# A one-core transformer step: rows of x saved earlier, state and gate transfers moved off a hand-over, a row chain spread over three pairs

## The reference, cut to what matters

```
x = x_sample + position table          (latent tokens only)
h = rms_norm(x) * (1 + scale1) + shift1         scale, shift, gate = silu(c) @ w_ada + b_ada
z = h @ w_in                                    branches A, B, C and their merge gates
y = (sig(gA)*A + sig(gB)*B + sig(gC)*C) @ w_out
x = x + gate1 * rms_norm(y)
h = rms_norm(x) * (1 + scale2) + shift2
a, b = h @ w_ffn_in ;  x = x + gate2 * rms_norm((silu(a) * b) @ w_ffn_out)
```

## Time and profile before

| | us |
|---|---|
| median of 3 runs | 1740.62 (1739.48 to 1744.54) |
| the profiled execution | 1741.52 |
| its span, first to last instruction | 1739.7 |
| PE busy | 1692.2 (97%) |
| DVE busy | 992.7 (57%) |
| ACT busy | 628.8 (36%) |
| POOL busy | 222.5 (13%) |
| granted TensorE clock, mean | 0.993 |

### The profile page before, as it was taken

How to read it: one execution, slowest core, us unless ns; L and a number is a source line. 1 busy time by engine, 2 the same in 40 slices (tenths; PEclk the granted TensorE clock), 3 DMA queues, 4 the chain that set the end, 5 groups by cost and what they waited for, 6 DMA issues and landing times. The chain is left out here.

```text
span 1739.7 us, 24679 instructions
## 1 busy us (share of the span) xinstructions
PE 1692.2 (97%) x9558; PEld 1601.8 (92%) x9558; DVE 992.7 (57%) x1674; ACT 628.8 (36%) x1102; POOL 222.5 (13%) x340
## 2 busy tenths in 40 slices
PE   6899999999999999999999899999999999999996
PEld 3799999989999999998988799999999999888885
DVE  5654443343444444456978886555555553589885
ACT  6311212242322222234667563222222222454452
POOL 1400001322222233311000000000000000000000
PEclk9999999999999999999999999999999999999998
DMA  9655445664455556679876322221122226567683
GB/s 349 234 176 186 163 150 198 227 201 140 165 173 172 186 190 206 198 253 274 265 234 192 141 101 81 76 67 70 60 75 76 76 76 193 152 198 240 187 277 124
DMA packets 155579, 295.74 MB, mean 170 GB/s; under 512 B 12761, under 2 KB 91932, under 8 KB 155466
## 3 DMA queue, kind: packets, MB, share of 16 engines
q1 hardware_dynamic: 111600, 162.69, 28.8%
q0 software_dynamic: 27536, 91.31, 16.0%
q10 hardware_dynamic: 16336, 40.29, 6.3%
HBM read 226.46 MB, written 67.82 MB: 169 GB/s over the span
## 5 line engine op out<-in xcount | busy, mean ns | idle before, releaser
L669 PE MATMUL bank<-h_hi,w_hi 128*128 128x384 f32 x1080 | 370.8, 343 | 7.5 <-DVE h_lo L2658 3.6
L671 PE MATMUL bank<-h_hi,w_lo 128*128 128x384 f32 x1080 | 362.0, 335 | 0.0
L670 PE MATMUL bank<-h_lo,w_hi 128*128 128x384 f32 x1080 | 361.7, 335 | 0.0
L1972 DVE TENSOR_TENSOR w_lo<-raw,w_hi 128x1024 fp32r<-128x1024 f32 x154 | 187.3, 1220 | 143.9 <-ACT w_hi L1482 143.8
L669 PEld LDWEIGHTS bank<-h_hi,w_hi 128*128 128x128 f32 x1080 | 203.4, 188 | 12.3 <-DVE h_lo L2658 5.8
L670 PEld LDWEIGHTS bank<-h_lo,w_hi 128*128 128x128 f32 x1080 | 203.6, 188 | 0.1
L671 PEld LDWEIGHTS bank<-h_hi,w_lo 128*128 128x128 f32 x1080 | 203.1, 188 | 0.0
L1482 ACT CAST w_hi<-raw 128x1024 fp32r<-128x1024 f32 x154 | 159.3, 1052 | 98.8 <-PE bank L671 43.2
L670 PE MATMUL bank<-w_lo,a_hi 128*128 128x512 f32 x352 | 136.9, 389 | 0.0
L671 PE MATMUL bank<-w_hi,a_lo 128*128 128x512 f32 x352 | 136.9, 389 | 0.0
L669 PE MATMUL bank<-w_hi,a_hi 128*128 128x512 f32 x352 | 136.9, 389 | 0.0
(11 more groups left out here) (358 smaller groups left out, 3375.7 us busy)
## 6 DMA issues: line engine op xcount, KB each, us to landing
raw<-in_w_stream SPq DMA_DIRECT2D x144, 512.0 KB, 4.5
z_scratch<-z_st ACTq DMA_DIRECT2D x44, 576.0 KB, 2.9
raw<-in_w_stream SPq DMA_DIRECT2D x90, 256.0 KB, 4.5
raw<-in_w_ada SPq DMA_DIRECT2D x35, 512.0 KB, 4.4
mg<-z_scratch ACTq DMA_DIRECT2D x24, 576.0 KB, 5.3
a_raw<-f_scratch SPq DMA_DIRECT2D x44, 256.0 KB, 3.8
a_raw<-f_scratch SPq DMA_DIRECT2D x22, 320.0 KB, 3.6
zt<-z_scratch POOLq DMA_DIRECT2D x27, 256.0 KB, 4.2
```

What stands on the lines that cost most here:

```text
L669: pe.matmul(out, a_hi, b_hi, start=start, stop=False)
L670: pe.matmul(out, a_hi, b_lo, start=False, stop=False)
L671: return pe.matmul(out, a_lo, b_hi, start=False, stop=stop)
L1972: dve.tensor_tensor(w_lo[:, slot], raw[:, slot], w_hi[:, slot].bitcast(F32), ALU.subtract).then_inc(s_wlo, 1)
```

## The change

- SP's first stream load of unit 1 keeps its place in time but is written into turn 0, and right behind it SP itself issues the nine stores of `x_in` (`x_stores`). POOL's nine stores and a wait before them are gone; POOL still waits for them to land.
- `mg_load(0)` and `mg_load(1)` move from part 2 of `hm`, ahead of pieces 2 and 3 of `mx`, to parts 3 and 4.
- The two stores of new_C move from POOL's place ahead of `mx_load(2)` to e2(0), beside those of new_n.
- `x_add(3g+1)` moves from the first unit of e1(g+1) to the end of e2(g).
- In e2(2) DVE splits the first feed-forward unit before `combine(0)` instead of after it, and makes `s_low(0)` before `t_low(4)`.
- The row chain of tiles 6 to 8 (`x_add`, `x_square`, `x_rstd`, `x_norm`) is spread from pair 0 over pairs 0 to 2, and POOL's `x1_store` of them comes behind the first stores of f.

```diff
+            def x_stores():
+                sp.wait_ge(s_padd, 2 * (LAT // P))
+                for c in range(NT):
+                    sp.wait_ge(s_xin[c], 16)
+                    sp.dma_start(xp_dram[c], x_in[:, c]).then_inc(s_xps, 16)
...
                     load((n0 + 2) % RAW, w_ada[bass.ds(i * (2 * RAW) + (ADA_FIRST + 2 * u + 1), 1)])
+                    if first and u == 0:
+                        sp.wait_ge(s_unit, n0 + 3 - RAW + 1)
+                        load((n0 + 3) % RAW, w_stream[1:2])
+                        x_stores()
...
-                        mg_load(0)
-                        mg_load(1)
+                    if part in (3, 4):
+                        mg_load(part - 3)
                     for k in MX_PARTS[part]:
                         mx_piece(0, k)
...
-                    if j == 0:
-                        x_square(6)
+                    if j == 1:
                         x_norm(6)
                     elif j == 2:
+                        x_norm(8)
                         h2_out(6)
...
-                    if j == 0:
+                    if j == 1:
                         x_square(7)
...
-                    if j == 0:
+                    if j == 1:
                         x_norm(7)
                     act.wait_ge(s_pv, vector_step(j, "c12"))
                     act.activation(v1[:, :], v1[:, :], ACT.Silu).then_inc(s_pact, 1)
-                    if j == 0:
-                        x_square(8)
-                        x_norm(8)
+                    if j < 2:
+                        x_square(6 + 2 * j)
...
-                    if g and c == 0:
-                        x_add(m + 1)
...
-                    if g < NG - 1 or k not in (3, 4):
+                    if g < NG - 1 or k not in (3, 4, 5):
                         split(n + AHEAD, n + AHEAD)
...
                             x_add(3 * g)
+                            x_add(3 * g + 1)
...
                             t_low(i)
+                        split(n + 2 + AHEAD, n + 2 + AHEAD)
                         combine(0)
                     elif k == 5:
+                        s_low(0)
                         t_low(4)
-                        s_low(0)
...
-                        x_add(6)
                     dve.wait_ge(s_pact, scalar_step(j, "s1"))
...
+                    if j == 1:
+                        x_rstd(6)
+                        x_add(7)
+                    elif j == 2:
+                        x_rstd(8)
...
-                    if j == 0:
-                        x_rstd(6)
-                        x_add(7)
...
-                    if j == 0:
-                        x_add(8)
+                    if j == 1:
                         x_rstd(7)
...
-                    if j == 0:
-                        x_rstd(8)
+                    if j < 2:
+                        x_add(6 + 2 * j)
...
-            pool.wait_ge(s_xr, NT)
-            for c in range(NT):
-                pool.dma_start(xp_dram[c], x_in[:, c]).then_inc(s_xps, 16)
             pool.wait_ge(s_xps, 16 * NT)
...
             hm_load(8)
-            for d in range(2):
-                pool.dma_start(new_C[0, 0, d].rearrange("h k v -> k h v"), st_ctx[:, d, :, 0:DH]).then_inc(s_new, 16)
             mx_load(2)
...
                     for d in range(2):
+                        pool.dma_start(new_C[0, 0, d].rearrange("h k v -> k h v"), st_ctx[:, d, :, 0:DH]).then_inc(s_new, 16)
...
-                    if j == 0:
-                        for m in range(6, 9):
-                            x1_store(m)
                     f_store(0, j, c21[:, :], s_pv, vector_step(j, "f1"))
                     f_store(1, j, v2[:, :], s_pv, vector_step(j, "f2"))
+                    if j == 0:
+                        x1_store(6)
+                    elif j == 1:
+                        x1_store(7)
+                        x1_store(8)
```

More of the change, by code:

```diff
@@ L788, in z1_turn @@
                     n0 = ADA_FIRST + 3 * u
[L789 to L793, removed]
+                    if not (first and u < 2):
+                        sp.wait_ge(s_arow, i * 32 + ada_done(u - 2, 1))
                         load(n0 % RAW, w_stream[bass.ds(i * RAW + u, 1)])
@@ L2317, in e1 @@
                     split(n + AHEAD, n + AHEAD)
-                    if g and c == 0:
-                        x_add(m + 1)
-                    elif g and c == 1:
+                    if g and c == 1:
                         x_rstd(m)
```

## The result

The changed kernel took 1727.6 us in the median of four runs (1724.1 to 1731.0), the kernel before 1741.1 beside it: a ratio of 0.992, 95% interval 0.989 to 0.995. The prediction said 1725.3. The profiled execution of the changed kernel is the slowest of the four, 1731.0 us with a span of 1729.2.

A forecast was written before the change was run, and what follows sets the result against it. PE was taken as the bound, busy 1692.2 of 1739.7 us, so only its stalls could go. 4.75 + 4.6 + 0 + 7.1 - 1.1 = 15.35 us gave 1725.3 us, range 1722 to 1732.

The forecast's parts named there:

- First stall, 4.75: Near 75 us: earlier stores of x let the stream load of unit 2 land in time, ending PE's w_lo wait; 4.75 us.
- The rival that the stores slow the making of h: At 42 to 61 us: store traffic slows DVE, ACT and POOL, making PE late; 1744 us at double length, chance 0.03.
- Hand-over, 4.6: Near 760 us: mx piece 2 lands sooner without new_C and gate loads ahead, ending PE's mx_lo wait; 4.6 us.
- The chain that I followed, 2, 4, 6: Hand-over: piece 2 releases 4, 4 releases 6; 11.1 us after piece 2 lands, piece 6 is ready, 1.9 us early.
- the rival: Hand-over keeps its stall because gate loads and the last hm_store meet pieces 4 and 6; 1730 us, chance 0.15.
- e2(2), 0: Last e2 stage into pair 0: PE starts without its 1.27 us wait but waits longer before product 6; gain 0.
- The gap of 2.4: Pair 0: PE waits 2.4 us before product 6 for y_scale(6); a clock fall there would cost 1.5 us.
- Row chain, 7.1 less 1.1 for the new wait: Pairs 0 to 2: spreading the chain ends PE's S_lo stall in pair 1, 7.1 us, less 1.1 us waited later.
- The new wait: Turn of tile 7: h2_out(6) waits for the stores of tiles 7 and 8, so PE waits 1.1 us, bounds 0 and 4.
- one of the prediction's own signs of being wrong: A PE wait over 2 us in pairs 1 to 3, or clock 0.50 anywhere from 60 to 1700 us.
- ACT 6.9 us late: Pairs 1 on: five table changes, each with a drain, put ACT 6.9 us later; about 1731 us, chance 0.05.
- Sum 15.35: Whole span: 4.75 + 4.6 + 0 + 7.1 - 1.1 = 15.35 us, taking the span from 1739.7 to 1724.3.

The follow-up runs named there:

- the hand-over alone: Kernel before with new_C behind the first x_load calls, gate loads in parts 3 and 4, x_add(3g+1) from e1 to e2: 1735.4 us, ratio 0.9969.
- the second trace: Profiled execution of the unaltered changed kernel, measured once more later: 1724.4 us, with a median of 1725.1 us, ratio 0.9916 to the kernel before.
- The parts alone: Stores of x, hand-over, e2(2) order and row chain, each changed alone on the kernel before: 1736.6, 1735.4, 1738.5 and 1736.2 us.

## Why the prediction was right, and where not

- **First stall, 4.75.** Right in mechanism and size, in both traces of the changed kernel and with the stores alone. The rival that the stores slow the making of h is refuted: with 0.96 instead of 0.11 of the DMA engines in use, PE needed the same time from 42 to 61.7 us, within 0.3, in both traces and with the stores alone.
- **Hand-over, 4.6.** The size was right (4.2 in the first trace, 4.5 in the second), the reason half right. I charged the delay of piece 2 to new_C and the gate loads together. new_C moved alone gave 4.7, the gate loads alone 0.4. The chain that I followed, 2, 4, 6, came out as forecast: 11.4 us instead of 11.1, with 1.8 in hand. What I left out is the chain 3, 5, 7. With the gate loads between the pieces it took 12.5 us instead of 10.8, as the rival had it in kind, and ended 0.26 us too late for PE. That the wait stayed this small is luck: it was 1.2 us with the hand-over alone and 0 in the second trace.
- **e2(2), 0.** The gap of 2.4 was forecast and measured as 2.6. The step that failed is "If it comes, it costs what nine slow matmuls cost in the earlier trace rows, 3.04 - 9 x 0.1735 = 1.5 us": it came in the first execution and cost 2.9, because the clock stayed low for longer than nine matmuls, up to about 978 us; in the second it did not come. The bound was too narrow above. With it came one of the prediction's own signs of being wrong, 0.50 of the clock between 60 and 1700 us. The 0 itself stands: with the old order the changed kernel took the same time (1724.6 against 1725.1), though not for the reason that I gave, but because the chain of DVE and ACT sets the turn either way.
- **Row chain, 7.1 less 1.1 for the new wait.** The stall for `S_lo` was gone in every kernel with the chain spread. The new wait is real but its size hangs on how early PE comes: 0 with the slow clock, 0.34 without, 2.0 when pair 0 runs through. What I did not see is that the same chain makes every gain in pair 0 worthless. Stretch against stretch: 54.7 to 48.2 is 6.5 us, where the sum had 6.0. The 7.1 is what the stall cost in before's trace; in three other traces it cost 5.7 to 5.9.
- **Table loads.** In the first trace after, the root starts right behind its load, as in the earlier trace rows; the drain of 1.38 us of the Trainium skill's "ScalarE: Activation LUTs", section "What ACT_TABLE_LOAD costs", is again not there, so the estimate made from it, ACT 6.9 us late, did not come true:

```profile
987.97 1.28 ACT L1718 ACT_TABLE_LOAD   x1
989.26 0.29 ACT L1718 ACTIVATE stat<-stat,eps 128x1 f32<-128x1 f32 x1
```

- **What the sum did not hold.** Sum 15.35 for the span; first trace 10.5, second 17.1; the medians fell by 13.5 and 14.5. (The parts alone fell by 3.5, 4.7, 1.1 and 3.8, together 13.0.) That the forecast came within 2.3 and 0.2 us of the two medians is in part luck: what two traces of the same kernel lose by chance differs by more than that. The first lost 1.4 by 25 us, 1.5 in the gates, 1.2 at `g_sb` and 2.9 at product 6. The first three are not the change's: at 61.7 us the fourteen traces lie from -1.3 to +1.4 us of before's, edited ahead of it or not, the 1.5 us in the gates are in 10 of the 13 traces other than before's, whatever was edited, and the wait for `g_sb` is 0.4 us or less in every other trace. Both medians lie between the two executions. What sets the clock off in the gates was not tried and stays open.

## What to carry to other kernels

Price a stall as its bracket plus the slow matmuls behind it, but treat the second part as something that comes in some executions and not in others. When a wait in front of one engine is removed, look for the next point at which that engine meets the same helpers: if their chain is full in between, the wait is only moved there, and an order that "gives PE its work earlier" is worth nothing. And if a transfer is late, see first who was issued just ahead of it; taking 1.5 us of issuing and 0.5 MB from in front of it gave all that was to be had, and moving 1.15 MB from beside it to between the pieces behind it gave next to nothing.

## What the runs showed of the hardware

- The same instructions with the same idle gap of 2.6 us had a granted clock of 0.62, then 0.70 behind it in one execution (2.9 us lost), 0.90 and 0.76 in another kernel (1.7), and 1.00 in a third trace (nothing).
- Nine stores of 512 KB took SP 5.98 us to issue at 42 us and 9.15 us at 64 us, where the DMA engines were full (1.01 of them in 65 to 70); the two loads behind took 1.25 and 1.20 us each to issue instead of 0.33:

```profile
65.00:70.00 5.00, 5.00 (x30) 5.00 (x29) 1.63 (x3) 0.00 (x0) 0.00 (x0) 1.00 1.01 404
```
